# Two transformer blocks in fp32 on one core: another order of the splits, squares and transposes at the head, in the first gated stage and in the final norm

## What is computed

```
def rms_norm(x, g):
    return x * rsqrt(mean(x * x, axis=-1) + EPS) * g

# block 1: x is (256, 1024)
h = rms_norm(x, g_mix);  proj = h @ w_in             # 1024 -> 8192 columns
... differential attention and retention on proj, then mixed @ w_out
h2 = rms_norm(x, g_mlp)
x = x + square(relu(h2 @ w_ff1)) @ w_ff2             # 4096 wide
gate_p = sigmoid(rms_norm(x, g_ple) @ w_ple_gate)
x = x + gate_p * (p @ w_ple)
x = rms_norm(x, g_final)
# block 2
x = x + 0.5 * swiglu(rms_norm(x, ffn1_norm), w_gate, w_up, w_down)     # 2816 wide
... two attentions on rms_norm(x, mix_norm) @ w_in2, joined @ w_out2
x = x + 0.5 * swiglu(rms_norm(x, ffn2_norm), w_gate2, w_up2, w_down2)
out = rms_norm(x, final_norm)
# swiglu(h) = (silu(h @ w_gate) * (h @ w_up)) @ w_down
```

## Time and profile before

| | us |
|---|---|
| median of 3 runs | 1019.09 (1019.06 to 1019.16) |
| the profiled execution | 1019.27 |
| its span, first to last instruction | 1017.3 |
| PE busy in the span | 995.5 (98%) |
| DVE busy | 571.9 (56%) |
| ACT busy | 504.7 (50%) |

### The profile page before, as it was taken

The page is one execution under the profiler, slowest core; times in us unless marked ns, Lnnn a source line. Parts: engine busy times, 40 slices in busy tenths (PEclk is TensorE's granted clock), DMA queues, the critical chain, the costliest instruction groups (busy, mean ns, idle before and its releaser), DMA issues.

```text
span 1017.3 us, 12900 instructions
## 1 busy us (share of the span) xinstructions
PE 995.5 (98%) x4744; PEld 821.1 (81%) x4744; DVE 571.9 (56%) x769; ACT 504.7 (50%) x700; POOL 63.9 (6%) x94
## 2 busy tenths in 40 slices
PE   8999999999999999999989999999999999999997
PEld 5888788888888888888778888888877888888885
DVE  5645555477675455545675455547555575555443
...
GB/s 352 228 166 166 165 166 152 149 129 165 167 255 194 178 195 166 205 169 185 184 140 204 173 200 179 193 147 167 175 204 63 44 187 184 197 176 204 169 122 42
DMA packets 98864, 175.63 MB, mean 173 GB/s; under 512 B 5936, under 2 KB 54016, under 8 KB 98816
## 3 DMA queue, kind: packets, MB, share of 16 engines
...
...
## 4 chain that ended last, share of the span: by engine, by line
PE 94%; DVE 3%; ACT 1%; issue 1%; POOL 1%; DVEq 0%; POOLq 0%; ACTq 0%
PE bank L496 85%; PE bank L510 5%; PE bank L555 1%; PE bank L554 1%; DVE w_lo L1375 1%; ACT hA_hi L986 0%; PE bank L566 0%; POOL ms L1875 0%; PE bank L607 0%; DVE hA_lo L1388 0%; PE bank L568 0%; PE bank L567 0%; PE bank L848 0%; PE bank L847 0%; PE bank L846 0%
## 5 line engine op out<-in xcount | busy, mean ns | idle before, releaser
L1375 DVE TENSOR_TENSOR w_lo<-raw,w_hi 128x2048 fp32r<-128x2048 f32 (+1 forms) x162 | 365.6, 2262 | 218.3 <-ACT w_hi L974 218.2
L974 ACT ACTIVATE w_hi<-raw 128x2048 fp32r<-128x2048 f32 (+1 forms) x162 | 306.4, 1894 | 153.2 <-PE bank L496 152.9
L496 PE MATMUL bank<-w_hi,hA_hi 128*128 128x512 f32 (+1 forms) x880 | 342.6, 395 | 6.9 <-DVE hA_lo L1388 2.6
L496 PE MATMUL bank<-w_hi,hA_lo 128*128 128x512 f32 (+1 forms) x880 | 336.6, 388 | 0.0
L496 PE MATMUL bank<-w_lo,hA_hi 128*128 128x512 f32 (+1 forms) x880 | 336.1, 388 | 0.0
L496 PEld LDWEIGHTS bank<-w_hi,hA_hi 128*128 128x128 f32 x880 | 164.9, 188 | 41.8 <-DVE hA_lo L1388 3.0
L496 PEld LDWEIGHTS bank<-w_hi,hA_lo 128*128 128x128 f32 x880 | 165.1, 188 | 34.7
L496 PEld LDWEIGHTS bank<-w_lo,hA_hi 128*128 128x128 f32 x880 | 165.4, 188 | 32.2
L496 PE MATMUL bank<-w_hi,fT_hi 128*128 128x512 f32 x304 | 93.9, 390 | 0.0
L496 PE MATMUL bank<-w_hi,fT_lo 128*128 128x512 f32 x304 | 93.6, 389 | 0.0
L496 PE MATMUL bank<-w_lo,fT_hi 128*128 128x512 f32 x304 | 93.6, 389 | 0.0
...
## 6 DMA issues: line engine op xcount, KB each, us to landing
raw<-in_w_in SPq DMA_DIRECT2D x74, 512.0 KB, 4.5
raw<-in_w_ff SPq DMA_DIRECT2D x64, 512.0 KB, 3.9
raw<-in_ffn_w_gate SPq DMA_DIRECT2D x44, 512.0 KB, 3.6
raw<-in_ffn_w_up SPq DMA_DIRECT2D x44, 512.0 KB, 4.5
raw<-in_ffn_w_down SPq DMA_DIRECT2D x44, 512.0 KB, 4.0
raw<-in_w_out SPq DMA_DIRECT2D x16, 512.0 KB, 4.2
raw<-in_w_branch_diff SPq DMA_DIRECT2D x8, 512.0 KB, 3.7
raw<-in_w_branch_ret SPq DMA_DIRECT2D x8, 512.0 KB, 3.7
```

Of the source, the lines that this page charges most:

```text
L496: mm = pe.matmul(o, a, w, start=first and t == 0 and m < len(outs), stop=last and t == n - 1 and m >= len(todo) - len(outs))
L974: act.activation(w_hi[u % HI_SLOTS][:, 0:w], raw[u % RAW_SLOTS][:, 0:w], ACT.Copy).then_inc(hi_ready, 1)
L1375: vec.tensor_tensor(w_lo[u % RAW_SLOTS][:, 0:w], raw[u % RAW_SLOTS][:, 0:w], w_hi[u % HI_SLOTS][:, 0:w].bitcast(f32), ALU.subtract).then_i ...
```

## The change

Four places, all of them the order or the banks of work that is already there, except for the last.

1. Head. PE turns the gain's rows before x's first half. DVE splits two of the four blocks of `hA`, then the weights' piece 1, then the other two blocks. PE turns x's last quarter (`mix_turn(1, 1)`) four products earlier, after two of row block 1's first four products; the other two, and two of row block 0, come after it now.
2. `ff_up0`, in all three stages that use it: the two transposes of row block 1 no longer stand together but two products apart, and the first block goes to banks 0 and 1. The wait for `up_out` ahead of the second block goes; it comes back ahead of the first sums into banks 0 to 3.
3. The first gated stage: PE's transposes of row block 0 one step earlier, after (1, 1). On ACT the split of row block 0 stands ahead of unit f1 + 1's high part and of the squares, `ple_gate(1)` ahead of `squares("ffn1", 0)`, and `squares("mid", 1)` behind the split of row block 1 and unit f1 + 2. On DVE the split of row block 0 stands ahead of `mid_norm(0)` and unit f1 + 1.
4. The end. The 24 last matmuls close one half, then the other. DVE adds a half, multiplies it by the gain into `xg`, and ACT squares a half into `ss2`; DVE joins the two sums to the mean, POOL only raises it to the power. ACT scales all of row block 0 and columns 640 to 1023 of row block 1, DVE columns 0 to 639 (`CUT`). There are three writes instead of four: 512 KB and 320 KB by SP, 192 KB by ACT.

The diff, cut to its core:

```
-    up = lambda tb: bank[4 + tb]
+    up = lambda tb, i=1: bank[4 + tb if i else tb]
@@ SP, the end
-        for n in range(2 * TB):
-            ... sp.wait_ge(src_ready, SRC["final"] + n + 1)
-            sp.dma_start(out_d[tb * P:(tb + 1) * P, cols], src[:, tb, cols]).then_inc(out_done, 16)
+        sp.wait_ge(scaled, 1)
+        sp.dma_start(out_d[0:P, :], src[:, 0, :]).then_inc(out_done, 16)
+        sp.wait_ge(src_ready, SRC["final"] + 1)
+        sp.dma_start(out_d[P:2 * P, 0:CUT], src[:, 1, 0:CUT]).then_inc(out_done, 16)
@@ PE, the head
+        pe.wait_ge(g_in[0], 16)
+        gain_turn(0)
...
                 mix_turn(0, 1)
-                products(sums[1], hA, 0, 4, 1, 0, HALF, True, False, operand="mix").then_inc(unit_used, 1)
-                products(sums[0], hA, 4, 2, 0, 1, HALF, False, False, operand="mix")
+                products(sums[1], hA, 0, 2, 1, 0, HALF, True, False, operand="mix")
                 mix_turn(1, 1)
-                products(sums[0], hA, 4, 4, 0, 1, HALF, False, True, t0=2, operand="mix").then_inc(proj_done, 1)
+                products(sums[1], hA, 0, 4, 1, 0, HALF, False, False, t0=2, operand="mix").then_inc(unit_used, 1)
+                products(sums[0], hA, 4, 4, 0, 1, HALF, False, True, operand="mix").then_inc(proj_done, 1)
@@ PE, ff_up0 (block 1's first wait below goes with it)
-            narrow_block(up(0)[:, :], norm, u0, 0, HALF, lambda: src_turn(norm, 1)).then_inc(up_done, 1)
-            narrow_block(up(1)[:, :], norm, u0, 1, HALF)
+            out = [up(0, 0)[:, :]]
+            products(out, hA, 0, 4, 0, u0, HALF, True, False, operand=norm)
+            turn_rows(norm, x, 1, (0,))
+            products(out, hA, 4, 2, 0, u0 + 1, HALF, False, False, operand=norm)
+            turn_rows(norm, x, 1, (1,))
+            products(out, hA, 4, 4, 0, u0 + 1, HALF, False, True, t0=2, operand=norm).then_inc(up_done, 1)
+            narrow_block(up(1, 0)[:, :], norm, u0, 1, HALF)
...
-                    if j == 0:
+                    if j == 0 and i > 1:
                         pe.wait_ge(up_out, 2 * steps - 1 + tb + 2 * di)
...
                         acc_free(name, tb)
+                        pe.wait_ge(up_out, 2 * base + 2)
@@ PE, the block ahead of the gated stage
-                       steps={(0, 1): lambda: src_turn("ple", 1), (1, 2): lambda: src_turn("ffn1", 0)})
+                       steps={(0, 1): lambda: src_turn("ple", 1), (1, 1): lambda: src_turn("ffn1", 0)})
@@ ACT, the first gated stage
         hi(U0["f1"])
         squares("mid", 0)
+        split_rows("ffn1", 0)
         hi(U0["f1"] + 1)
+        ple_gate(1)
         squares("ffn1", 0)
-        split_rows("ffn1", 0)
-        ple_gate(1)
+        split_rows("ffn1", 1)
         hi(U0["f1"] + 2)
         squares("mid", 1)
-        split_rows("ffn1", 1)
@@ ACT, the end
+        half_square(0)
+        act.wait_ge(x_gain, 2)
+        act.activation(src[:, 0, :], xg[:, 0, :], ACT.Copy, scale=inv_rms("final", 0)).then_inc(scaled, 1)
+        act.wait_ge(half_squared, 1)
+        half_square(1)
+        act.wait_ge(x_gain, 4)
+        act.activation(src[:, 1, CUT:D], xg[:, 1, CUT:D], ACT.Copy, scale=inv_rms("final", 1)).then_inc(scaled, 1)
+        act.wait_ge(scaled, 2)
+        act.dma_start(out_d[P:2 * P, CUT:D], src[:, 1, CUT:D]).then_inc(out_done, 16)
@@ POOL, the end
+        pool.wait_ge(mean_ready, 1)
+        pool.tensor_tensor(rs[:, n + 1:n + 2], ms[:, n + 1:n + 2], nhalf[:, 0:1], ALU.pow).then_inc(rstd_ready, 1)
```

More of the change, by code:

```diff
@@ L38 @@
 WARM = (7, 4)
+CUT = 640
 DH, DHD = 8, 64
@@ L205, in two_blocks @@
     g_col = sb("g_col", [P, 96])
+    ss2 = sb("ss2", [P, 4])
     at[0] = -(-at[0] // LINE) * LINE
@@ L1466, in _ @@
         vec.wait_ge(g_ready, 1)
-        split(("mix", 0, 0))
+        low_blocks(("mix", 0, 0), (0, 1))
         first_piece(1)
+        low_blocks(("mix", 0, 0), (2, 3))
         first_piece(2)
@@ new lines, in by_gain @@
+            def by_gain(tb, c):
+                cols = slice(c * HALF, (c + 1) * HALF)
+                vec.tensor_tensor(xg[:, tb, cols], x[:, tb, cols], gain[:, cols], ALU.mult).then_inc(x_gain, 1)
+            sums_ready("f2", 0)
+            add(0, 0)
+            add(0, 1).then_inc(acc_out, 1)
+            vec.wait_ge(gain_in, GAIN["final"])
+            vec.wait_ge(acc_out, 2 * ACC["f2"] + 1)
+            for c in range(2):
+                by_gain(0, c)
+            for c in range(2):
+                vec.wait_ge(last_half, c + 1)
+                add(1, c).then_inc(half_added, 1)
+                if c:
+                    vec.wait_ge(half_squared, 1)
+                    vec.tensor_scalar(ss2[:, 2:3], ss2[:, 0:1], 1.0 / D, EPS, ALU.mult, ALU.add)
+                vec.wait_ge(half_added, c + 1)
+                by_gain(1, c)
```

83 lines of the change are left out of this document (49 added, 34 removed).

## The result

| | before | after |
|---|---|---|
| median of 6 runs | 1019.10 (1018.84 to 1019.19) | 1013.08 (1012.67 to 1013.20) |
| the profiled execution's span | 1017.3 | 1011.1 |
| PE busy in the span | 995.5 | 994.5 |

The ratio is 0.994, 95% interval 0.993 to 0.9949. The time fell by 6.0 us; 5.8 had been forecast. The span is 6.2 shorter. The starts of the same matmuls in the two traces divide this among the three places: 2.15 in the head, 2.9 in the first gated stage, 1.2 behind the last matmul.

What follows compares the result with a forecast made beforehand. PE, busy 995.5 of 1017.3 us, was taken as the bound, so only its waits and the end pay: 1.95 + 2.7 + 1.15 = 5.8 us off 1019.27 gives 1013.5, median 1013.3 us, range 1012.1 to 1015.9.

Steps and rivals of the forecast that it cites:

- The head: Start of the kernel: three PE waits, at 9.18, 18.59 and 22.34, go; 1.95 us gained, bounds 0.95 to 2.1.
- idle plus 0.16: Reading rule for every matmul wait: its cost is the idle in brackets plus 0.16 us.
- The cover by the transfer: Head: unit 2's 512 KB land at 14.7, just ahead of 15.1, when ACT's split before its high part ends.
- The gain's term: Head: gain's transpose ahead of x's first half, taken as 0; may gain 0.1 or lose up to 1.0 us.
- rival B: Head: the gain's rows land late and hold x's first transposes; up to 1.0 us back, 1014.3; chance 0.08.
- The other users of `ff_up0`: Two other stages: PE never stands, idle ACT and DVE absorb later splits; 0 each, 0 to 0.5 us lost otherwise.
- The gated stage: First gated stage: 5.1 us of waits replaced by a new 2.1 and small ones; 2.7 gained, bounds 1.6 to 3.2.
- rival A: First gated stage: longer chain, new wait 3.2 to 3.6 instead of 2.1 us, banks bring next to nothing; 1014.8; chance 0.12.
- The hold on POOL: First gated stage: POOL's mean held again under DVE's low parts, `act_f` at about 523.6, PE waits 0.35 us.
- The end: Behind the last matmul: shorter chain to the last write, 1015.8 against 1016.9; 1.15 us saved, bounds 0.5 and 1.8.
- Rival C: Last writes: the one on ACT's queue takes 3.4 us, so 0.7 more, 1014.0; chance 0.06.
- Rival E: Gated stage: the 2.1 us wait drops PE's clock to 1.2 GHz; 8 us of such work gives 1021.3; chance 0.02.

Runs made afterwards that it cites:

- experiment 1: Changed kernel with the head of the kernel before (gain's transpose, low parts and x's last quarter as they were); median 1015.26 us.
- experiment 10: Changed kernel with only the gain's transpose put back behind x's first half; median 1013.02 us.
- experiment 3: Changed kernel with all `ff_up0` blocks in banks 4 and 5 and the wait ahead of the second block, order kept; median 1018.17 us.
- experiment 4: Changed kernel with the whole of `ff_up0` as before: banks 4 and 5 and row block 1's eight transposes together; median 1016.13 us.
- experiment 2: Changed kernel with the first gated stage's old order on PE, ACT and DVE, banks 0 and 1 and parted transposes kept; median 1013.07 us.
- experiment 7: Changed kernel with the low part of f1 + 2 ahead of `mid_norm(1)` on DVE in the first gated stage; median 1014.21 us.
- experiment 8: Changed kernel with `silu(0, 1)` and `multiply(0, 1)` of the first gated stage ahead of f1 + 4's high and low part; median 1013.00 us.
- experiment 9: Changed kernel with the edits of experiments 7 and 8 together; median 1010.68 us, ratio to the kernel before 0.991.
- experiment 11: Changed kernel with `CUT` at 1024: DVE scales all of row block 1, SP writes it in one 512 KB piece; median 1013.21 us.
- experiment 12: Kernel of experiment 9 with `CUT` at 768: 384 KB written by SP, 128 KB by ACT; median 1010.86 us.
- experiment 5: Changed kernel with one more unused square on ACT ahead of f1 + 2's high part, lengthening PE's wait at the second block; median 1015.48 us.
- experiment 6: Changed kernel with the end of the kernel before (`final_norm`, its sums, two DVE scalings, four SP writes); median 1014.29 us.

## Why the prediction was right, and where its steps were not

**The head** (1.95 forecast, 2.15 measured). All three waits went, and experiment 1 gives them back in full. The rule "idle plus 0.16" was a little short: behind each wait the next matmul starts 0.33 after the first (18.93 after 18.59 before), not 0.23, so each wait costs 0.1 more than I counted. That holds for the last two; of the wait for piece 1, 0.15 stayed, and its slower start with it: I had called it gone, but two blocks of `hA_lo` and the piece still end at 8.4. The cover by the transfer held: ACT began unit 2 at 14.91 with no bracket. The gain's term, taken as 0, can't be told from 0 by experiment 10; rival B fell.

**The other users of `ff_up0`** (0 forecast, 0 measured). Here the result hides two terms of 1.15: taking the transposes apart would have cost 0.45 and 0.7, the banks cover them (experiments 3 and 4). My reason, the idle time of ACT and DVE in the whole stretch, was an average and missed the one moment: the second block waits for `act_f` out of the same bank, and that is exactly what the later split delays. The number was right by the banks, which I had not priced there at all.

**The gated stage** (2.7 forecast, 2.9 measured). The walk was right nearly step by step. The new wait ends with the low part at 515.3, which is 517.5 in the time of before (2.2 later by the head), and I had 517.6; it lasts 1.88 and not 2.1, since PE came 0.15 later: my 515.5 left out most of the wait of 0.3 for `x` that stands in the same walk (503.5 + 0.3 + 11.84 = 515.64), and that wait was there (504.30). `act_f(0, 1)` ends at 521.31, or 523.5, and I had 523.6; the small wait is 0.3 and not 0.35. What failed is the account that I gave of it: "So of the 5.1 us of waits 526.6 - 523.9 = 2.7 are gained" reads as if the order had removed the waits at the start and the banks, at best, the later ones, with only the weight unit behind them. The experiments split it otherwise. With banks and parted transposes but the old order the time is the same, 1013.07 (experiment 2); with the order alone, 0.4 is lost, 1.1 gained in waits and 1.6 lost to the clock (experiment 4). Nearly all of the 2.9 hangs on the banks: without them the stage is 3.95 longer (experiment 3), 1.6 of it by the clock, so the rest of the change is worth 0.6 there by its waits, or 1.1 with the transposes together. And the walk's last step is the one that sets the end: `act_f(0, 1)`, late through POOL. The wait for the low part runs beside it and is worth nothing by itself (experiment 7), and this one 0.3 (experiment 8); together they are 2.3 (experiment 9). In rival A I wrote that a later chain would mean that the banks "brought next to nothing". That is wrong in its sense too: with the late unit and without the banks PE stands 4.5 us (experiment 3), or 3.1 (experiment 4), instead of 1.88.

The hold on POOL was in the walk and came, though not where it was before: the power, and not the mean as in the kernel before, was held the longest: it began at 515.40 and ended at 517.87, where the second low part on DVE had ended at 517.5, and the product at 517.95 to 520.2, where DVE's next low part ended at 520.2. In experiment 7 the same power, while DVE idled, took 0.55. This is how the Trainium skill ("SBUF — State Buffer", "Who interferes with whom") describes a pair of ports that DVE and GpSimd share as an exclusive lock; the trace agrees, 2.47 against 0.55 us for an operation on 128 x 1.

**The end** (1.15 forecast, 1.2 measured). The steps: add 0.69 as forecast, half a square and its sum from 1005.76 to 1006.49, the mean to 1006.75, the power to 1007.37, DVE's scaling 0.55 against my 0.53, ACT's end at 1008.08, 0.1 behind DVE's and not "no later", and the writes at 2.2 and 2.6 against 2.7 after issue. Rival C (a write of 3.4 on ACT's queue) fell: 192 KB took 2.6 there. Experiments 11 and 12 show that neither the number of writes nor the cut matters by more than 0.1; what gained was the chain ahead of them, half an add and half a square instead of whole ones and one scaling with one operand (0.75 for 1024 columns against 1.42 before).

**Rival E**, the lower clock, had 0.02, because "for it speaks nothing in the rows". As a forecast of the median that was right: all six runs of the changed kernel had 0.998 or 0.999. As a statement on the mechanism it was too light. A wait only 0.95 us longer (experiment 5) brings it in the profiled execution, and where a trace shows a fall it costs about 1.6 us (experiments 3, 4, 5 and 8). Whether the changed kernel's own wait of 1.88 ever brings it is not shown: its six executions had none, the kernels of experiments 1, 6, 8, 10 and 11, which have the same wait, show a lower mean clock in 4 of 24, and the one place seen is another (experiment 8). The kernels of experiments 2, 9 and 12, without that wait, show it in none of 14. The price in my rival, 12 us of lower clock to cancel the gain, was far off what happens: it lasts some 3 to 3.5 us. The Trainium skill ("TensorE: Matmul & The Clock Gate", "What's actually happening") has the clock fall after idle time and come back with work; the trace agrees, 0.50 in the granted clock for the matmuls from 519.28 to 522.27 behind a wait of 4.49, and 0.23 from start to start again after that.

**Left open**: what the banks bring without the transposes taken apart, what moves the first product between 7.16 and 7.91, and whether the length of a wait alone or also the waits shortly before it decide on the clock; the stretch at 801 to 808 in experiment 8 speaks for the second, but it is one trace.
